# Retention stage: the key and output transposes alternate between two PSUM banks, key tokens are copied out between the query columns, the first head's values go to the spare buffer, and the first row numbers of the experts are copied early

## What is computed

```python
scores = jnp.einsum('bnihd,bnjhd->bnhij', qc, kc) * intra[None, None]
o_intra = jnp.einsum('bnhij,bnjhe->bnihe', scores, vc)
kv = jnp.einsum('bnjhd,bnjhe->bnhde', kc * k_dec[None, None, :, :, None], vc)
...
o_cross = jnp.einsum('bnihd,bnhde->bnihe', qc * q_dec[None, None, :, :, None], s_in)
```

## Time and profile before

| what | value |
|---|---|
| median of 3 runs | 1921.36 us (1915.17 to 1923.42) |
| profiled execution, its own time | 1921.21 us |
| its span | 1919.5 us |
| PE busy | 1778.6 us, 93% of the span |
| mean granted clock of PE | 0.971 |
| DVE, ACT, POOL busy | 54%, 41%, 26% |
| memory traffic over the span | 168 GB/s |

### The profile page before, as it was taken

The page is one execution under the profiler, slowest core; times in us unless marked ns, Lnnn a source line. Parts: engine busy times, 40 slices in busy tenths (PEclk is TensorE's granted clock), DMA queues, the critical chain, the costliest instruction groups (busy, mean ns, idle before and its releaser), DMA issues. The chain is left out here.

```text
span 1919.5 us, 25622 instructions
## 1 busy us (share of the span) xinstructions
PE 1778.6 (93%) x10100; PEld 1551.7 (81%) x10100; DVE 1041.5 (54%) x1192; ACT 781.8 (41%) x943; POOL 503.9 (26%) x285
## 2 busy tenths in 40 slices
PE   5999999999999999999999979929999999999992
PEld 5999989998999999999999968717777776667661
DVE  5555680001455444554511143256898887888884
ACT  5455460000122111221300032226787877778774
POOL 1323332223222322222222210022333332224210
PEclk9999999999999999999999989959999999999996
DMA  4211011223111111111132466327999999999995
GB/s 130 61 50 50 28 56 57 78 67 112 47 36 33 36 37 45 36 33 36 47 101 90 156 206 227 148 96 260 374 379 368 373 374 359 365 362 380 373 331 196
DMA packets 146085, 316.17 MB, mean 165 GB/s; under 512 B 10652, under 2 KB 106092, under 8 KB 121292
## 3 DMA queue, kind: packets, MB, share of 16 engines
q1 hardware_dynamic: 136140, 288.27, 41.7%
q0 software_dynamic: 9856, 26.66, 5.2%
HBM read 287.46 MB, written 35.29 MB: 168 GB/s over the span
## 5 line engine op out<-in xcount | busy, mean ns | idle before, releaser
L220 PE MATMUL job_ps<-xn_hi,w_hi 128*128 128x352 f32 x1536 | 511.6, 333 | 7.9 <-ACT ret_v_features L1017 4.7
L222 PE MATMUL job_ps<-xn_hi,w_lo 128*128 128x352 f32 x1536 | 494.9, 322 | 0.0
L221 PE MATMUL job_ps<-xn_lo,w_hi 128*128 128x352 f32 x1536 | 494.5, 322 | 0.0
L220 PEld LDWEIGHTS job_ps<-xn_hi,w_hi 128*128 128x128 f32 x1536 | 290.0, 189 | 11.6 <-issue 7.9
L204 POOL CAST w_hi<-w_raw 128x1024 fp32r<-128x1024 f32 x80 | 88.2, 1103 | 784.8 <-issue 465.9
L221 PEld LDWEIGHTS job_ps<-xn_lo,w_hi 128*128 128x128 f32 x1536 | 290.5, 189 | 2.3
L222 PEld LDWEIGHTS job_ps<-xn_hi,w_lo 128*128 128x128 f32 x1536 | 289.9, 189 | 0.0
L2054 DVE TENSOR_TENSOR ex_w_lo<-u,ex_w_hi 128x2048 fp32r<-128x2048 f32 x96 | 217.8, 2285 | 26.2 <-ACT ex_w_hi L1964 26.2
L2054 DVE TENSOR_TENSOR ex_w_lo<-h_raw_more,ex_w_hi 128x2048 fp32r<-128x2048 f32 x96 | 217.8, 2286 | 20.5 <-ACT ex_w_hi L1964 20.5
L206 POOL TENSOR_TENSOR w_lo<-w_raw,w_hi 128x1024 fp32r<-128x1024 f32 x80 | 215.5, 2693 | 6.4
L1964 ACT ACTIVATE ex_w_hi<-u 128x2048 fp32r<-128x2048 f32 x96 | 184.2, 1921 | 71.2 <-DMA u<-in_w_chunks 27.3
(11 more groups left out here) (279 smaller groups left out, 3049.4 us busy)
## 6 DMA issues: line engine op xcount, KB each, us to landing
u<-in_w_chunks SPq DMA_DIRECT2D x96, 1024.0 KB, 16.6
h_raw_more<-in_w_chunks SPq DMA_DIRECT2D x96, 1024.0 KB, 17.1
w_raw<-in_w_in SPq DMA_DIRECT2D x64, 512.0 KB, 4.1
merged_lru<-gate SPq DMA_DIRECT2D x8, 528.0 KB, 4.7
spare<-merged_lru SPq DMA_DIRECT2D x8, 528.0 KB, 5.5
merged<-gate SPq DMA_DIRECT2D x8, 528.0 KB, 4.8
x_tile<-in_x_prompt SPq DMA_DIRECT2D x8, 512.0 KB, 4.7
w_raw<-in_w_lru_o SPq DMA_DIRECT2D x8, 512.0 KB, 3.9
```

The lines of the kernel that those rows point to most:

```text
L220: pe.matmul(out, M.w_hi[s][:, k, :], x_hi[:, k, cols], start=(k == 0), stop=False)
L221: pe.matmul(out, M.w_hi[s][:, k, :], x_lo[:, k, cols], start=False, stop=False)
L222: mm = pe.matmul(out, M.w_lo[s][:, k, :], x_hi[:, k, cols], start=False, stop=(k == KD - 1))
```

## The change

Retention's small work changes its order and its banks. In the loop, one part of "ot" and one of "kt" now alternate, so that all of "ot" is on bank 0 and all of "kt" on bank 1. The copy of k's transposed tokens, which ACT did after all three query columns, is now done between the columns. For the first head, ACT takes v into the spare buffer, and only behind that waits for the stage before. The last head's last output part moves one column on. In `experts`, the first two row numbers are copied before the first gather is issued, and DVE waits for both before its first low part.

```diff
 class Turns:
-    ORDER = (("sc", 1), ("sc", 2), ("o", 0), ("o", 1), ("o", 2), ("vt", 0), ("vt", 1), ("vt", 2), ("ot", 0), ("ot", 1),
-             ("kt", 0), ("ot", 2), ("kt", 1), ("kt", 2), ("kv", 0), ("kv", 1), ("kv", 2), ("sc", 0))
+    ORDER = (("sc", 1), ("sc", 2), ("o", 0), ("o", 1), ("o", 2), ("vt", 0), ("vt", 1), ("vt", 2), ("ot", 0), ("kt", 0),
+             ("ot", 1), ("kt", 1), ("ot", 2), ("kt", 2), ("kv", 0), ("kv", 1), ("kv", 2), ("sc", 0))
...
         def v_turned(kind, h, c):
             if c == 0:
                 J.taken(pe, *v_at(kind, h))
-            turn_to(pe, kind, h, "vt", c, v_f, True)
+            turn_to(pe, kind, h, "vt", c, v_f if kind == "loop" else srg, True)
...
             def behind_q(c):
-                if kind == "loop":
-                    out_turned(kind, h, h - 1, c)
+                if kind == "loop" and c == 0:
+                    out_turned(kind, h, h - 1, 0)
                 if c:
                     k_turned(kind, h, c - 1)
+                    if kind == "loop":
+                        out_turned(kind, h, h - 1, c)
...
     def last_turned(pe, c):
-        if c == 1:
-            pe.wait_ge(on_done, HEADS)
-            for x in range(3):
-                turn_to(pe, "last", HEADS, "ot", x, on, False)
+        for x in ((), (0, 1), (2,))[c]:
+            if x == 0:
+                pe.wait_ge(on_done, HEADS)
+            turn_to(pe, "last", HEADS, "ot", x, on, False)
...
             earlier("vt")
-            take(*v_at(kind, h), v_f, ACT.Copy)
+            take(*v_at(kind, h), v_f if kind == "loop" else srg, ACT.Copy)
+            if kind == "first":
+                merged_before(act)
...
-            take(0, h * 2 + 1, q_f, ACT.Copy)
-            earlier("kv")
-            if kind == "first":
-                act.wait_ge(table_in, 32)
-            for c in range(3):
+            def take_k_t(c):
+                if c == 0:
+                    earlier("kv")
+                    if kind == "first":
+                        act.wait_ge(table_in, 32)
                 bank, free = turns.ready(act, kind, h, h, "kt", c)
...
+            take(0, h * 2 + 1, q_f, ACT.Copy, lambda c: take_k_t(c - 1) if c else None)
             if kind == "loop":
                 act.wait_ge(u_done, h * 3)
-            take(1, h * 2 + 1, srg, ACT.Silu)
-
-        earlier.last_product(act)
-        earlier.all_stored(act)
-        act.wait_ge(init, 1)
+            else:
+                act.wait_ge(turns.done["vt"], 3)
+            take(1, h * 2 + 1, srg, ACT.Silu, lambda c: take_k_t(2) if c == 0 else None)
+
+        def merged_before(eng):
+            earlier.last_product(eng)
+            earlier.all_stored(eng)
+            eng.wait_ge(init, 1)
...
                 pool.wait_ge(router.slots_done, 1)
+                rows_of(0)
+                rows_of(1)
                 load(0)
                 load(1)
...
                 router.vector(dve)
+                dve.wait_ge(row_set, 2)
                 for c in range(3):
                     lo(0, c)
```

More of the change, by code:

```diff
@@ L757 @@
 class Turns:
-    ORDER = (("sc", 1), ("sc", 2), ("o", 0), ("o", 1), ("o", 2), ("vt", 0), ("vt", 1), ("vt", 2), ("ot", 0), ("ot", 1),
-             ("kt", 0), ("ot", 2), ("kt", 1), ("kt", 2), ("kv", 0), ("kv", 1), ("kv", 2), ("sc", 0))
-    FIRST = ORDER[5:8] + (ORDER[10],) + ORDER[12:]
-    LAST = ORDER[0:5] + ORDER[8:10] + (ORDER[11],)
+    ORDER = (("sc", 1), ("sc", 2), ("o", 0), ("o", 1), ("o", 2), ("vt", 0), ("vt", 1), ("vt", 2), ("ot", 0), ("kt", 0),
+             ("ot", 1), ("kt", 1), ("ot", 2), ("kt", 2), ("kv", 0), ("kv", 1), ("kv", 2), ("sc", 0))
+    FIRST = ORDER[5:8] + ORDER[9:14:2] + ORDER[14:]
+    LAST = ORDER[0:5] + ORDER[8:13:2]
     def __init__(self, nc, ctx, keep, R):
@@ L771, in at @@
     def at(self, kind, h, stage, c):
-        bank_of = {place: i % 2 for i, place in enumerate(self.ORDER)}
+        in_loop, bank_of = ({place: i % 2 for i, place in enumerate(some)}
+                            for some in (self.ORDER, self.LAST if kind == "last" else self.ORDER))
         places = {"first": self.FIRST, "loop": self.ORDER, "last": self.LAST}
         bank = bank_of[stage, c]
-        used = lambda some: sum(bank_of[p] == bank for p in some)
+        used = lambda some: sum(in_loop[p] == bank for p in some)
         mine = places[kind]
-        before = used(mine[:mine.index((stage, c))])
+        before = sum(bank_of[p] == bank for p in mine[:mine.index((stage, c))])
         if kind != "first":
@@ L1784, in _, with rows_of @@
             def _(pool):
+                def rows_of(e):
+                    if e >= ROWS:
+                        pool.wait_ge(y_added, 16 * (e - ROWS + 1))
+                    pool.tensor_copy(row[e % ROWS][:], H.slots[:, e:e + 1]).then_inc(row_set, 1)
                 def load(e):
@@ L1788, in load @@
                         pool.wait_ge(x_turned, 2 * (e - XE) + 2)
-                    if e >= ROWS:
-                        pool.wait_ge(y_added, 16 * (e - ROWS + 1))
-                    pool.tensor_copy(row[e % ROWS][:], H.slots[:, e:e + 1]).then_inc(row_set, 1)
+                        rows_of(e)
                     pool.wait_ge(row_set, e + 1)
```

## The result

The changed kernel takes 1906.8 us (median, 1904.17 to 1908.51) against 1920.3 for the kernel before in the same runs: ratio 0.9929, 95% interval 0.9915 to 0.9943, 13.5 us faster. The forecast was 1905.4. The sum was nearly right, but only because its errors cancel: of its four terms one came out an eighth short, one at less than half, one with the wrong sign, and one that was to be zero was 6 us.

What follows compares the result with a forecast made beforehand. PE was taken to bound the kernel, busy 93% of the span. Terms of 7.5 + 8.2 + 0.15 + 0 = 15.9 us off the profiled 1921.2 gave 1905.4 us, range 1897 to 1911.

Steps and rivals of the forecast that it cites:

- First head: Retention's first head: waits for v and key tokens go, with a slow clock; gain 7.5 us (5.8 to 8.3).
- I add about one us: First head: POOL's split starts only near the rotation's end, so the rotation takes 6.1 us instead of 5.1 undisturbed.
- a sign of being wrong: First head: a low clock there still would show the forecast wrong; no size given.
- Loop: Seven retention heads: the key-token wait behind the third query column goes, 7 x 1.17 = 8.2 us (7.4 to 11.6).
- seven waits of 0.5 us for the bank's release: Loop, behind the second query column: seven waits of about 0.5 us for L1098's release, now before an output transpose.
- End of retention: Last head's output: the 1.94 us wait goes but the part comes a column later; gain 0.15 us (-0.5 to 1.9).
- ends the last at 957.3: End of retention: DVE starts blocks 4 to 7 at 952.5, 1.19 us each, and ends the last at 957.3.
- Row numbers: Start of experts: faster row-number copies, but the first gather lands about as before; gain 0 us (-0.6 to 0.5).
- the gather gets through: Rival, start of experts: low parts don't hold up the gather, up to 6.3 us more, 1899.0 us; chance 0.13.
- With three in its way it ends at 1283.05: Start of experts: the first gather, beside three DVE low parts, ends at 1283.05, against 1283.49 before.
- this rival: Expert stage takes the gain back, and more, as weight loads don't keep up; up to 1931 us; chance 0.04.
- the loop gives nothing: Rival: in the loop DVE's release holds PE instead of ACT's wait; 1913.5 us; chance 0.15, including half the gain.

Runs made afterwards that it cites:

- split_late_first: Changed kernel, but in the first head POOL splits the gate weights only once k is rotated: 1903.5 us, ratio 0.9907.
- order_alone: Changed kernel, but ACT copies all three key-token parts after the third query column, as before; the alternating transposes stay: 1917.2 us, ratio 0.9989.
- copy_alone: Kernel before, with only ACT's order changed: key tokens copied behind the second and third query column and the first gate activation: 1914.5 us, ratio 0.9967.
- split_late_all: Changed kernel, but in every head POOL splits the gate weights only once k is rotated: 1894.6 us, ratio 0.9872.
- end_as_before: Changed kernel, but at the end of retention all three output parts are turned behind the second column, as before: 1900.4 us, ratio 0.9905.
- rows_alone: Kernel before with the row-number edit only (both copies ahead of DVE's low parts, DVE waits for them): 1915.2 us, ratio 0.9977.
- ret_alone: Changed kernel without the row-number edit, with the new retention: 1912.0 us, ratio 0.9954.
- gather_first: Changed kernel, but DVE's low parts wait for a POOL signal placed behind the first gather; it came 0.18 us before the gather began: 1907.1 us, ratio 0.9936.
- copy_behind_gather: Changed kernel, but the second row number is copied behind the first gather instead of ahead of it: 1902.7 us, ratio 0.9900.
- best: Changed kernel with gate-weight splits after k's rotation, blocks 4 and 5 before the third gated part, next split held, second row number behind first gather: 1890.4 us, 0.9842.
- rows_unheld: Changed kernel without DVE's wait for the two row numbers, POOL's new order kept: 1911.7 us, ratio 0.9956.
- end_low_first: Changed kernel, but at the end of retention DVE makes the low parts of blocks 4 to 6 before gating the third part: 1903.8 us, ratio 0.9911.

## Why the prediction was right in sum and wrong in its steps

**First head: 7.5 us forecast, 3.5 measured.** The wait for v is gone, and the start of the rotation (471.5 forecast, 471.86 measured) and the gone wait for key tokens are as said. The step that failed is "I add about one us" for POOL's split beside the rotation. It was drawn from the time at which I thought the split would start. It started at 473.75, and its two parts lie beside the last two steps, which took 2.7 us more than 1.26 each. With that the stop was 3.13 us instead of 0.9, and the clock, which no longer fell at 461, fell behind this stop, which I had listed only as a sign of being wrong. split_late_first shows both: with the split held, stop and slow stretch go, 4.5 us. The first head would then have given 8.0 us, what I forecast and a little more.

**Loop: 8.2 us forecast, 7.1 measured**, 1.01 us a head for 1.17. The mechanism is as predicted, and order_alone and copy_alone pin it to ACT's copy. Behind the third query column PE lost 1.93 us and now loses 0.86 (the rest of both is transposes), so the wait and its overlap make 1.07, not 1.17. The 0.3 us of later DVE work did not matter. The loss behind the second column stayed, as said (1.62 us before and after), but not with the sign that I gave for it: in place of seven waits of 0.5 us for the bank's release, the key transpose waits 0.3 us for the rotation itself, and the output transpose takes the rest. I took that wait as given. split_late_all shows that POOL's split causes it: without the split beside the rotation it goes, 0.7 us a head.

**End of retention: a gain of 0.15 us forecast, a loss of 4.2 measured.** Failed step: "ends the last at 957.3", four low parts of 1.19 us. I took their price from the rows of before, where POOL was idle beside them. Behind the third column, though, PE has finished the product in whose buffer POOL writes, and the split starts at that moment (941.36, with the third transpose at 941.13). By taking the third part a column later, the change put the low parts exactly beside it. end_as_before, where the start is 2.2 us earlier against PE, shows 5.1 us for the place. In it too the low parts are slowed (5.61 us), but they lie early enough. The trace of before had such a price on the same line L730: its eight low parts for "ml", with a split of POOL at 279.39 beside them, take 12.44 us from 273.65 on, and not 8 x 1.25 = 10.0. How large the loss is depends on the clock as well: the same stretch took 167.2 us before, but 168.8 in rows_alone, which has the old order too and whose clock fell there.

**Row numbers: 0 forecast, 6.4 measured** (5.9 by rows_alone). The rival "the gather gets through" is what happened to the time, though not for its reason. The gather was held up, but by one low part. The step that failed is "With three in its way it ends at 1283.05". I took the 5.34 us of the earlier trace rows, a gather beside two low parts, as the rule. It is one of 32 gathers, in the trace of the kernel before as in that of the changed one (first and second line); in the latter the others end 0.85 to 0.91 us behind one low part, or take about 1.0 us:

```profile
L1793 POOL DMA_INDIRECT ex_rows<-xf_rows,ex_row x32: 977/2815/5343, 1282.5 to 1838.3; - x32
L1807 POOL DMA_INDIRECT ex_rows<-xf_rows,ex_row x32: 982/2823/5338, 1269.2 to 1825.1; - x32
```

(the numbers are minimum, median and maximum in ns). So the row was a single case, and the grouped view of this one line in the trace of before says so. It would not have given the right number: nearly all the other gathers have one low part beside them, and not three on end. What it should have changed is the chance of the rival.

**Experts and the rest.** From the first turned rows to the last it is 563.2 us before and 563.3 after, and from the first turned rows to the end of the span all fourteen traces lie between 627.4 and 630.1 us, whatever was gained ahead: a gain won ahead of the stage passes through, and this rival is out. So is "the loop gives nothing".

**Sum.** The terms were off by -4.0, -1.1, -4.3 and +6.4 us, and 1.5 us came from elsewhere; together -1.5. None of the four lies within the bounds that I gave it. That the forecast hit is luck: without the row numbers it would have been 1912.0 (ret_alone), just outside the range.

## What to carry to other kernels

A wait that is removed gives what the next late thing allows, and that thing's duration has to be taken beside the work that it will then lie beside: here POOL's weight splits, which made DVE steps of 1.26 us into 3.3. Before a duration from one place is used in another, look at all instances of its line (minimum, median, maximum), and ask of each moved piece what starts at the same moment. Keeping two engines apart by one wait a head of the one that has slack, POOL, was worth nearly as much as the whole change (10.5 us by the traces, 12.2 by the medians, against 13.5). And to divide a gain among places, measure between instructions that keep their place in the order.

## What the runs showed of the hardware

**DVE and POOL hold each other up, in both directions.** With both inputs in SBUF, a DVE step of 1.26 us takes up to 3.3 beside POOL's split, and the split 3.26 instead of 2.38. The Trainium skill ("SBUF — State Buffer", Who interferes with whom) says that issue order decides who blocks. In part the trace agrees: a gather whose low part begins 0.07 us later takes 1.00 us (below), one that begins 0.18 us behind it 3.03 (gather_first). Where both begin within 0.01 us, both happen: 3.15 us for the gather at 1386.49 of the changed kernel, 1.00 for that at 1618.95.

```profile
1638.51 1.00 POOL L1807 DMA_INDIRECT ex_rows<-xf_rows,ex_row  x1 [0.81 <-POOL ex_row L1799]
...
1638.58 2.29 DVE L2070 TENSOR_TENSOR ex_w_lo<-h_raw_more,ex_w_hi 128x2048 fp32r<-128x2048 f32 x1 [0.33 <-ACT ex_w_hi L1980]
```

The Trainium skill's inference that writing descriptors is not held up by such a DVE instruction does not carry over to an indirect DMA: the instruction as a whole is held up wherever a low part began 0.1 us or more before it and still ran (2.42 us in changed, 3.03 in gather_first, against 1.04 with DVE idle). Whether it is held in writing its descriptors or in reading its row numbers, which lie in SBUF, no run separates.

**Over how many back-to-back low parts POOL is held is open.** A gather begun 0.78 us behind the start of a low part was let through after that one, one begun in the same instant (1296.72) only after the second, and a copy begun 0.24 us behind only after the third, in three runs. I tried no run that separates these.

**The first gather lands later when weight chunks are out.** From the end of its issue to the transpose it took 3.2 us with no chunk issued since the slots (copy_behind_gather, best), 5.7 to 6.1 with a 1 MB chunk issued 0.9 us ahead of its end (changed, gather_first, rows_alone), and 5.7, 6.7 and 7.1 with three of them ahead (ret_alone, rows_unheld, before). The first step is clear of the scatter, the second is not.

**The clock.** PE had full-rate work on both sides of these stops. Stops of 1.94 us, 1.95 (copy_alone), 2.17 (end_as_before) and 2.19 us (end_low_first) were not followed by a lower granted clock; those of 2.57 us and more, up to 4.70, had one in them or behind them, in every trace that has them. But rows_alone has the stop of 1.95 us too, and there the clock was at 0.50 behind it (the 1.2 GHz level):

```profile
949.59 0.21 PE L866 MATMUL ret_turn<-const,ret_out_tokens 32*128 32x32 f32 x1 [1.95 <-DVEq L1098]
...
950.50:953.40 2.90, 2.90 (x11) 2.90 (x11) 2.90 (x3) 2.87 (x4) 0.00 (x0) 0.50 0.56 186
```

So the length of the stop alone does not decide. Nor does it give the price: at the three places shown further up it was 0.50 for 3.3 to 3.4 us, which cost about 1.4 us each, but behind the 4.7 us stop of copy_alone for 6.6 us, and there the way to the first key transpose was 1.3 us longer than before. So of two traces that do the same up to a place, one can have the fall and the other not, and a difference of 1.5 us between two traces can be no more than that. What decides these rows don't say.
